# A retention computed from its scores alone, an opening inside the first stage, and a last projection closed tile by tile

## The reference, cut to what matters

```
o[t] = sum over s <= t of g^(t - s) * (q[t] . k[s]) * v[s]
```

## Time and profile before

| What | Value |
|---|---|
| median of 3 runs | 2789.81 us |
| profiled execution, its own time | 2789.72 us |
| its span, first to last instruction | 2787.9 us |
| mean granted TensorE clock | 0.993 |
| TensorE busy / weight loads | 98% / 80% |
| VectorE, ScalarE, GpSimd busy | 49%, 36%, 47% |
| TensorE idle before its first product | 11.2 us |
| DMA, mean | 103 GB/s |

### The profile page before, as it was taken

The page is one execution under the profiler, slowest core; times in us unless marked ns, Lnnn a source line. Parts: engine busy times, 40 slices in busy tenths (PEclk is TensorE's granted clock), DMA queues, the critical chain, the costliest instruction groups (busy, mean ns, idle before and its releaser), DMA issues. The chain is left out here.

```text
span 2787.9 us, 39696 instructions
## 1 busy us (share of the span) xinstructions
PE 2723.1 (98%) x16792; PEld 2234.2 (80%) x16792; DVE 1377.2 (49%) x1705; ACT 1005.1 (36%) x1391; POOL 1303.4 (47%) x923
## 2 busy tenths in 40 slices
PE   8999999989999999999999999999999999999997
PEld 6888887778888888777888888887888778888786
DVE  6863237674475436765515333115577654233422
ACT  4233234253333322446413433222326633222542
POOL 4545444634555544575445455444345434333343
PEclk9999999999999999999999999999999999999998
DMA  6644232101433323222223333335655312222232
GB/s 202 188 126 146 94 100 79 47 4 41 139 125 117 108 94 94 84 83 91 89 93 98 92 98 98 99 98 168 203 145 169 125 61 91 72 67 67 69 98 76
DMA packets 115218, 288.42 MB, mean 103 GB/s; under 512 B 34832, under 2 KB 46032, under 8 KB 114384
## 3 DMA queue, kind: packets, MB, share of 16 engines
q1 hardware_dynamic: 115040, 285.87, 32.9%
HBM read 261.94 MB, written 26.25 MB: 103 GB/s over the span
## 5 line engine op out<-in xcount | busy, mean ns | idle before, releaser
L430 POOL TENSOR_TENSOR weight_ring_r<-weight_ring,weight_hi_r 128x512 fp32r<-128x512 f32 (+2 forms) x824 | 1182.0, 1456 | 1362.4 <-ACT weight_hi_r L422 1357.6
L422 ACT ACTIVATE weight_hi_r<-weight_ring 128x1024 fp32r<-128x1024 f32 (+2 forms) x412 | 448.2, 1088 | 1464.3 <-PE acc L634 1102.3
L628 PE MATMUL acc<-p_r,weight_hi_r 128*128 128x512 f32 x1712 | 672.2, 393 | 12.7 <-ACT weight_hi_r L422 11.2
L629 PE MATMUL acc<-scr_r,weight_hi_r 128*128 128x512 f32 x1120 | 438.0, 391 | 0.0
L634 PE MATMUL acc<-p_r,weight_ring_r 128*128 128x512 f32 x1712 | 420.6, 389 | 0.0
L629 PE MATMUL acc<-p_r,weight_hi_r 128*128 128x512 f32 x1008 | 392.2, 389 | 0.0
L628 PEld LDWEIGHTS acc<-p_r,weight_hi_r 128*128 128x128 f32 x1712 | 322.5, 188 | 82.9 <-ACT weight_hi_r L422 11.7
L634 PEld LDWEIGHTS acc<-p_r,weight_ring_r 128*128 128x128 f32 x1712 | 321.4, 188 | 66.7
L629 PEld LDWEIGHTS acc<-scr_r,weight_hi_r 128*128 128x128 f32 x1120 | 211.5, 189 | 45.6 <-issue 2.6
L629 PEld LDWEIGHTS acc<-p_r,weight_hi_r 128*128 128x128 f32 x1008 | 189.2, 188 | 39.0
L628 PE MATMUL acc<-scr_r,weight_hi_r 128*128 128x512 f32 x544 | 219.2, 403 | 0.0
(11 more groups left out here) (565 smaller groups left out, 3932.3 us busy)
## 6 DMA issues: line engine op xcount, KB each, us to landing
weight_ring<-in_weights SPq DMA_DIRECT2D x372, 512.0 KB, 3.5
weight_ring<-in_weights SPq DMA_DIRECT2D x32, 704.0 KB, 4.0
weight_ring<-in_weights SPq DMA_DIRECT2D x8, 640.0 KB, 3.8
s_inner<-p SPq DMA_DIRECT2D x16, 256.0 KB, 4.4
s_outer<-p SPq DMA_DIRECT2D x16, 256.0 KB, 2.9
s_inputs<-p SPq DMA_DIRECT2D x16, 256.0 KB, 2.8
p<-s_inputs SPq DMA_DIRECT2D x8, 512.0 KB, 5.4
p<-s_inner SPq DMA_DIRECT2D x8, 512.0 KB, 8.2
```

What stands on the lines that cost most here:

```text
L422: self.nc.scalar.activation(self.r.weight_hi[:, ahead, 0:width], self.weight_ring[:, r, 0:width], ACT.Copy)\
L430: ins = self.nc.gpsimd.tensor_tensor(rest, raw, hi, ALU.subtract)
L628: pe.matmul(product.out(b, m), hi, op.hi(kx), start=sub == 0 and k == 0, stop=False)
L629: pe.matmul(product.out(b, m), hi, op.lo(kx), start=False, stop=False)
```

## The change

Three edits. **The start:** the block of its own is gone; SyncE issues the loads at the head of the first stage, in smaller pieces and another order (the first norm's gains alone, x chunk by chunk, slot 0 in two halves), TensorE first makes 12 products of ones with ones whose result nobody reads, the first slot is worked by halves and chunk by chunk, the second chunk by chunk; three of the seven additions of squares go to GpSimd, and the sum of squares moves into the third slot. ScalarE still rounds x chunk by chunk, with the halves of slot 0 after chunks 0 and 1 and slot 1 after chunk 3; VectorE follows it. **The retention:** the state is gone; step n makes the score products with all n + 1 key chunks up to its own, ScalarE scales the n earlier ones (`far_scores`), VectorE masks the own one, and `mixed` is n + 1 products with the values. **The end:** `closing_slot` finishes the first tile of the last slot before the second; chunk 7 is added and squared in two halves of tokens.

```diff
+            opening = product.first == 0 and b == 0
+            order = [(m, k) for k in range(g.kc) for m in range(g.mb)] if opening else [(m, k) for m in range(g.mb) for k in range(g.kc)]
...
+                if close is not None and s == product.end - 1:
+                    self.closing_slot(pe, product, close)
+                    yield b * g.q + sub
+                    continue
+                if s == 0:
+                    self.opening.pe_slot(pe, product)
+                    yield 0
+                    continue
...
+                for m, k in order:
+                    kx = product.input_part(b, sub) * g.kc + k
+                    if b == 0 and m == 0:
+                        pe.wait_ge(self.input_split, product.inputs + kx + 1)
...
+                if between is not None and b * g.q + sub == between[0]:
+                    between[1](pe)
...
+        for m in range(g.mb):
+            w_at = lambda k: slice(k * g.cols + m * P, k * g.cols + m * P + P)
+            for k in range(g.kc):
+                hi = self.r.weight_hi[:, s % AHEAD, w_at(k)]
+                pe.matmul(product.out(b, m), hi, op.hi(at + k), start=False, stop=False)
+                pe.matmul(product.out(b, m), hi, op.lo(at + k), start=False, stop=False)
+            if m == 0:
+                pe.wait_ge(self.weights_split, s + 1)
+            for k in range(g.kc):
+                mm = pe.matmul(product.out(b, m), self.r.weight_ring[:, s % RING, w_at(k)], op.hi(at + k), start=False, stop=k == g.kc - 1)
+            mm.then_inc(self.products_done if m else first_done, 1)
...
+    def sp_loads(self, sp):
+        core = self.core
+        vectors, gain = core.dram["vectors"], slice(0, DC)
+        sp.dma_start(core.vec[:, gain], vectors[:, gain]).then_inc(self.gain_loaded, 16)
+        self.load_x(sp, 0)
+        self.load_half(sp, 0, self.half_loaded)
+        self.load_x(sp, 1)
+        self.load_half(sp, 1, core.slot_loaded[0])
+        self.load_x(sp, 2)
+        self.load_x(sp, 3)
+        core.one_load(sp, 1, 1, core.width_of(1), None)
+        for k in range(4, DC):
+            self.load_x(sp, k)
+        sp.dma_start(core.vec[:, DC:], vectors[:, DC:]).then_inc(self.vec_loaded, 16)
+        for n in range(2, RING):
+            core.one_load(sp, n, n, core.width_of(n), None)
+        core.next_consts(sp, self.block0)
+
...
+    def pe_wake(self, pe):
+        core = self.core
+        pe.wait_ge(self.constants, 1)
+        for _ in range(WAKE):
+            pe.matmul(core.acc[:, BANKS - 1, 0:P], core.ones[:, :], core.ones[:, :], start=True, stop=True)
...
+        for half, rounded, split in ((0, self.half_rounded, self.half_split), (1, core.weights_rounded, core.weights_split)):
+            pe.wait_ge(rounded, 1)
+            chunks = range(half * g.kc // 2, (half + 1) * g.kc // 2)
+            for k in chunks:
+                pe.wait_ge(core.input_split, k + 1)
+                for m in range(g.mb):
+                    hi = core.r.weight_hi[:, 0, w_at(m, k)]
+                    pe.matmul(product.out(0, m), hi, op.hi(k), start=k == 0, stop=False)
+                    pe.matmul(product.out(0, m), hi, op.lo(k), start=False, stop=False)
+            pe.wait_ge(split, 1)
+            for m in range(g.mb):
+                for k in chunks:
+                    mm = pe.matmul(product.out(0, m), core.r.weight_ring[:, 0, w_at(m, k)], op.hi(k), start=False, stop=False)
+        mm.then_inc(core.products_done, 1)
...
-    norm1.adds = DC - 1
-    up_part = SwigluPart(core, "ffn1_up", up, norm1, down, lambda n: h[:, n, :])
+    norm1.adds = DC // 2
+    pool_sums = core.sem("ffn1_pool_sums")
+    up_part = SwigluPart(core, "ffn1_up", up, norm1, down, lambda n: h[:, n, :], root_at=2)
...
+                    if product is up and at == 0:
+                        for c in range(1, DC // 2):
+                            pool.wait_ge(squared, c + 1)
+                            if c > 1:
+                                pool.wait_ge(pool_sums, c - 1)
+                            nc.gpsimd.tensor_tensor(square(0), square(0), square(c), ALU.add).then_inc(pool_sums, 1)
...
+            core.opening.pe_wake(pe)
             steps = side()
-            for product, norm in ((up, norm1), (down, None), (mix, norm2)):
-                for at in core.flow_products(pe, product):
-                    if at == (1 if product is up else 0) and norm is not None:
-                        norm.pe_sum(pe)
+            for product in flow.products:
+                for at in core.flow_products(pe, product, between=(2, norm1.pe_sum) if product is up else None):
...
+            for n, c in enumerate((*range(DC // 2 + 1, DC), 0)):
                 dve.wait_ge(squared, c + 1)
-                if c > 1:
-                    dve.wait_ge(norm1.added, c - 1)
-                v.tensor_tensor(norm1.total, square(0) if c == 1 else norm1.total, square(c), ALU.add).then_inc(norm1.added, 1)
+                if c == 0:
+                    dve.wait_ge(pool_sums, DC // 2 - 1)
+                if n:
+                    dve.wait_ge(norm1.added, n)
+                v.tensor_tensor(norm1.total, norm1.total if n else square(DC // 2), square(c), ALU.add).then_inc(norm1.added, 1)
...
-                for j in range(2):
-                    ins = mm(scores, key(hd, j)[:, at], query(hd, j)[:, at], start=(j == 0), stop=(j == 1))
...
+                    pe.wait_ge(q["far"], earlier(i - 1))
+                for m in range(n + 1):
                     for j in range(2):
-                        ins = pe.transpose(keys_turned[:, j * P:(j + 1) * P], key(hd, j)[:, at], core.eye[:, :])
+                        ins = mm(scores(m) if m < n else own_scores, key(hd, j)[:, m * CH:(m + 1) * CH], query(hd, j)[:, at], start=(j == 0), stop=(j == 1))
...
+                pe.wait_ge(q["far"], earlier(i))
...
-                if n:
-                    pe.wait_ge(q["state"], updates(i - 1))
-                    for j in range(2):
-                        mm(o_bank, query(hd, j)[:, n * CH:(n + 1) * CH], state[:, j, :], start=(j == 0), stop=False)
-                mm(two(o_bank), st(i), value_at(hd, n), start=(n == 0), stop=True).then_inc(q["o"], 1)
-                if n < NCH - 1:
-                    if i:
-                        pe.wait_ge(q["copied"], i)
-                    pe.wait_ge(q["kd"], updates(i))
-                    for j in range(2):
-                        ins = mm(two(added[:, j, :]), kd(i)[:, j * P:(j + 1) * P], value_at(hd, n), start=True, stop=True)
-                    ins.then_inc(q["su"], 1)
+                pe.wait_ge(q["st"], i + 1)
+                for m in range(n + 1):
+                    ins = mm(two(o_bank), st(i, m), value_at(hd, m), start=(m == 0), stop=(m == n))
+                ins.then_inc(q["o"], 1)
 
...
-                pe.wait_ge(q["state"], updates(i))
...
+            pe.wait_ge(last_part.squared, DC - 1)
+            final.pe_add(pe, last_part.squares[0], 0, range(NCH), False, False)
             for n in range(2):
-                pe.wait_ge(last_part.squared, DC - 1 + n)
-                final.pe_add(pe, last_part.squares[n], 0, False, n == 1)
+                pe.wait_ge(last_part.squared, DC + n)
+                final.pe_add(pe, last_part.squares[1], 0, range(2 * n, 2 * n + 2), False, n == 1)
...
+            def far_scores(i):
+                hd, n = divmod(i, NCH)
                 act.wait_ge(q["scales"], 1)
-                act.wait_ge(q["st"], i + 1)
-                a(kd(i), keys_turned, ACT.Copy, scale=col(kdr, i)).then_inc(q["kd"], 1)
+                act.wait_ge(q["scores"], i + 1)
+                for m in range(n):
+                    a(st(i, m), scores(m), ACT.Copy, scale=col(far[n - m - 1], NCH * hd + m)).then_inc(q["far"], 1)
...
+                if at < last.n - 1:
+                    last_part.act_slot(act, at)
+            act.wait_ge(final.added, DC - 2)
+            act.wait_ge(ended, 1)
+            a(last_part.squares[0], x[:, DC - 2, :], ACT.Square).then_inc(last_part.squared, 1)
+            for n, at in enumerate(token_halves):
+                act.wait_ge(ended, n + 2)
+                a(last_part.squares[1][:, at], x[:, DC - 1, at], ACT.Square).then_inc(last_part.squared, 1)
...
-                if n < NCH - 1:
-                    dve.wait_ge(q["su"], updates(i))
-                    if n == 0:
-                        v.tensor_copy(state, added).then_inc(q["state"], 1)
-                    else:
-                        v.scalar_tensor_tensor(out=state, in0=state, scalar=C("chunk_decay")[:, hd:hd + 1], in1=added, op0=ALU.mult, op1=ALU.add).then_inc(q["state"], 1)
-                    dve.wait_ge(q["state"], updates(i))
...
-            for b in range(last.blocks):
+            for b in range(last.blocks - 1):
                 last_part.dve_block(dve, b)
+            dve.wait_ge(first_done, 1)
+            v.tensor_tensor(x[:, DC - 2, :], x[:, DC - 2, :], last.out(last.blocks - 1, 0), ALU.add).then_inc(ended, 1)
```

(3 more changed lines are left out.)

172 lines of the change are left out of this document (104 added, 68 removed).

## The result

The changed kernel takes 2774.26 us (median of 4 runs, 2771.65 to 2778.21), the kernel before, on the same chip, 2789.37 (4 runs, 2787.13 to 2791.67): a ratio of 0.9947, interval 0.9935 to 0.9959. That is 15.1 us less, where 19.1 were forecast. The four runs lie in two pairs, near 2771.8 and near 2777.4, and the profiled one (2776.63, span 2774.8) belongs to the slower pair. A later measurement of the same kernel, beside some of the experiments, gave 2772.59 (5 runs), 17.5 us less. So 15 to 17.5 us is what there is to explain, and the profile of that second measurement is needed beside the first.

What follows compares the result with a forecast made beforehand. TensorE, busy for 98% of the span, was taken to bound the kernel. Retention 8.7, start 8.1 and end 2.3 summed to 19.1 us off 2789.72, giving 2770.6 us; the range for 8 in 10 was 2765.5 to 2776.5.

Steps and rivals of the forecast that it cites:

- the likeliest case: Whole kernel: all three edits pay as forecast, 2770.6 us, own spread 2767 to 2774; chance 0.58.
- Retention, 8.7: Retention: 12.3 us less work on TensorE, 3.6 given back in waits, so 8.7 us won.
- The wait at n = 0: Retention, i = 4: TensorE waits 1.2 us for VectorE's norming, 0.8 more than before, three times.
- The wait at n = 1: Retention: TensorE waits 0.4 us for the norming where it waited for nothing, three times.
- The rival of dearer score products: Retention: score products cost 0.305 us each in long bursts; it gives 4.9 us, time 2774.4; chance 0.06.
- End, 2.3: Kernel's end: 4.57 us from first addition to inversion becomes 2.2, so 2.3 us won; bounds 1.5 and 2.8.
- Start, 8.1: Start: the third slot ends at 25.7 us instead of 33.8, so 8.1 us won.
- GpSimd's three additions ... hidden: Start: additions between rests of slots 1 and 2 end at about 19 us; slot 2's rests are due at 23.
- The rival of late data: Start: x arrives 5 us later than forecast, the start gives 3 us, time 2775.7; chance 0.16.
- The root's thin cover: Start: after the sum at 23.0 us the banks are free at 30.1; slot 4 wants them at 31.1.
- The products of ones: Start: 12 products take 5.4 us, hidden by the chunks' pace; without them a cold TensorE falls 2 to 4 us behind.
- rival of a falling clock: Retention: each of six waits brings low clock costing 3.4 us, 20.4 in all; time 2791.0, slower; chance 0.02.

Runs made afterwards that it cites:

- the run with the rests later: Changed kernel with all additions of squares on VectorE, their sum's product behind the third slot, GpSimd's second-slot rests after VectorE's x splits: 2771.65 us.

## Why the prediction was right and where it was wrong

The direction, the range and the likeliest case held: 2774.26 (and 2772.59) in 2765.5 to 2776.5. The sum was 2 to 4 us too good, and its terms fared like this.

- **Retention, 8.7: measured 9.1 to 9.2.** The count of work was right: with all waits taken away the retention is 13.2 us shorter than before, which is the 12.3 of work and the old waits of 0.3 to 0.4 at three places. The wait at n = 0 was forecast as 1.2 and measured 1.2 by what its removal gave. The wait at n = 1 was forecast as 0.4 and measured 0.16. The rival of dearer score products is refuted: 0.22 us each in bursts of eight and twelve instructions (four and six products). The ratio of the Trainium skill, "TensorE: Matmul & The Clock Gate", section "Back-to-back issue gap", would have made them 0.33, by the estimate in the prediction; the trace does not agree.
- **End, 2.3: measured 2.5** in the profile, by the steps named. No run has this edit alone.
- **Start, 8.1: measured 5.4 in the first profile and 3.9 to 5.1 in the others.** This is the term that was mis-sized. It failed at "chunks 4 to 7 are ready at 13.2, 14.4, 15.5 and 16.7" and at "GpSimd's three additions ... hidden". The first split began 0.5 to 1.8 us late, behind the loads. Then the row of VectorE's splits in the kernel before (6.84 / 6 = 1.14 us) was read as a duration. It is a mean of splits alone (0.75) and splits beside GpSimd (1.2 to 1.9). (Of its six, 1.48, 1.76 and 1.76 ran beside GpSimd's rests, and three of 0.74 after them.) The new order puts GpSimd's rests beside the first two of the four splits that TensorE waits for and the moved additions beside the others, so that they took 1.6 each as a rule. The forecast had 0.7 as a bound, on the good side, and no bound on the other. GpSimd's additions were forecast to end at 19 and ended at 21.56 (began at 16.75). The third slot's rests came behind them and were done by 24.96, before TensorE took them at 26.13; what held TensorE (0.54 us) was the sum, late because VectorE's own additions took 1.66 us each beside GpSimd.
- **The rival of late data** had a part of the truth (some 1.2 us), but not its price of 5, nor its reason: larger pieces did not help. The forecast gave the loads ahead the full 438 GB/s, and the queues moved 309 in those microseconds.
- **The root's thin cover** was seen rightly: 0.9 us were left in the changed kernel, and when the third slot came earlier it was the next stall in line (0.8 us).
- **The products of ones**: their length (5.4 us) and what they do to the spacing were right, their worth was not. It is nothing measurable.
- **The clock in the retention** did not fall, at three waits of a microsecond. The forecast's rival of a falling clock took its price from the earlier trace rows, "TensorE idle for 1.3 of 5 us". But the wait there was longer, with most of it ahead of that window, as the kernel before shows:

```profile
2171.27 2.08 PE L663 MATMUL acc<-scr_r,weight_ring_r 128*128 128x512 f32 x4 [4.57 <-POOL weight_ring_r L430]
```

  So that row was no measure of what a wait of one microsecond does. What the runs have is the wait of 0.98 us near 2338: low clock behind it in one profile of seven.

## What to carry to other kernels

Before work is moved to a second engine, look up in the trace how long the first engine's instructions take while the second one runs and while it stands still; a mean over both hides that moving an addition to GpSimd can cost VectorE what it saves. Where a wait follows from the order in one engine's queue, ask whether what stands ahead is urgent: the rotation was not, and swapping two calls gave 4 us, as much as the whole new opening (3.9 to 5.4). Cut a long kernel's profile at fixed points of the program and compare the pieces; here that gave the retention as 9.1 or 9.2 us in three profiles, where the median of the run with that edit alone gave 6.4 to 13.4, and it showed 4 us that came and went with the clock in parts that nobody had touched.

## What the runs showed of the hardware

VectorE's instructions with two inputs in SBUF are slowed by GpSimd, those that read PSUM are not. In the retention of the changed kernel:

```profile
2456.49 2.54 POOL L430 TENSOR_TENSOR weight_ring_r<-weight_ring,weight_hi_r 128x512 fp32r<-128x512 f32 x2 [4.01 <-ACT weight_hi_r L422]
2457.08 0.68 DVE L4332 TENSOR_TENSOR scr<-acc,cst 128x512 f32<-128x512 f32 x1
2457.80 1.79 DVE L4336 TENSOR_TENSOR p<-scr 128x512 f32<-128x512 f32 x1
2459.51 0.68 DVE L4337 TENSOR_TENSOR p<-scr 128x512 f32<-128x512 f32 x1
```

L4332 reads PSUM (acc) and takes 0.68 us beside GpSimd's halves; L4336 reads two tiles of SBUF and takes 1.79 beside them; L4337, the same operation, takes 0.68 when GpSimd has just ended. GpSimd pays too when VectorE's instructions follow one another: two halves took 2.54 us here, as much as with VectorE idle (2.52 at 2462.92), and 2.99 to 3.44 beside the rows of splits and additions in the opening. One input in SBUF is no safe sign either: a TENSOR_SCALAR of 128x64 with a single one (L1380 of the kernel before, at 47.58) took 1.18 us beside GpSimd's halves, and the next of the same shape (L1381) 0.20; one of 128x1024 took 0.74 alone (at 66.08 in the kernel before) and 1.78 beside GpSimd (at 63.39 in the run with the rests later). The Trainium skill, "SBUF — State Buffer", section "Who interferes with whom", says that a VectorE instruction with two SBUF inputs contends with a GpSimd instruction that reads SBUF, and calls the port pair that they share an exclusive lock. This case's traces agree for the instructions with two inputs, and in the size: L4336 took 1.1 us more, near the 1.27 of the GpSimd half (2.54 / 2) beside which it ran nearly from start to end.

The granted clock was 0.59 over the 5 us (2160 to 2165) in which a gap of 5.7 us ends, and 1.00 there when the gap held 20 products of ones. But it also fell behind waits of 2.1 and 1.0 us in one profile and not in the next of the same kernel. The low stretches come at few places, much the same from profile to profile (near 520 to 560, 600, 1220, 1885, 2165 us and at the end; 2230 and 2340 in one profile alone); each costs 1.7 or 3.4 us, by clock lost times its length. The Trainium skill, "TensorE: Matmul & The Clock Gate", section "What's actually happening", says of the rise at a kernel's start that its point varies. No run here shows why the stretches vary, only that they come and go, with up to 6 us between two profiles in parts that no edit touches.
